# A hybrid decoder step on one core: the triangular inverse of the gated-delta mixing loop grown in place, and its TensorE work reordered

## The chip, the cores and the metric

The kernel runs on one core of one Trainium2 chip. The metric is the device time of one execution in microseconds (us), lower is better. All data is float32.

## What is computed

One layer for 1024 prompt tokens and 8 sampled tokens: RMSNorm, one input projection, two groups of mixing heads (sliding-window attention with 8 query and 2 key heads; a gated DeltaNet with 8 heads of width 64), output projection and residual, a mixture of experts, a gated embedding, a last norm. The change is in the prompt's mixing, and there in the DeltaNet, per head and per chunk of 64 tokens:

```
gam   = cumsum(g)
decay = exp(where(causal, gam_i - gam_j, -inf))
A     = where(strict, (k*beta) k^T * decay, 0)
sol   = triangular_solve(I + A, [v*beta, k*beta*exp(gam)])       # u, w
v_new = u - w S
o     = (q*exp(gam)) S + where(causal, q k^T * decay, 0) v_new
S     = S*exp(gam_last) + (k*exp(gam_last - gam))^T v_new
```

## The kernel before

The program has stages, each a block of five engine programs that meet at semaphores: projection and convolution (to about 360 us), mixing (365 to 899), routing and experts (to 1357), the last stage. The mixing stage works on tiles of 128 prompt tokens. A tile holds two chunks of 64 tokens, one in the lower and one in the upper 64 partitions (`HB`), and all 8 heads stand side by side (slots of 64 columns). The first tile is written out ahead of the loop (`first=True`; it also carries the output projection of the 8 sampled tokens), the other seven are one loop body, `Fori(1, NT)`, on every engine.

The body is skewed. Attention scores, decay sums, Gram matrices and the inverse are those of tile t; the end of the DeltaNet of tile t-1 (`solve_first`, `carry`, `solve_second`, `outputs`, `increments`, `turn_out`) and the output projection of tile t-1 (`project`, 8 parts k, each 128 rows of the weight for two times 512 columns) stand between them. A hand-written order on TensorE (from L1430) is what places the work; the other engines' orders are written to match. Semaphores count once per tile or per level, and eight PSUM banks are shared by hand.

In each tile, of what the change touches:
- TensorE computes the running sums of g into banks 4 to 6 (L1443 to L1445). VectorE subtracts them (L1178, `E_`), GpSimd adds a mask of -1e30 (L1038), ScalarE takes the exponential (L1306).
- q and k are turned to token rows (L1451), squared on ScalarE (L1299), summed and completed on VectorE (L1183 to L1186); GpSimd raises 16 columns to -0.5 (L1027, `rms_pow("qk")`).
- VectorE forms `gU = E_ * bet` (L1198), and `ATd`, the two 64x64 diagonal blocks of the transposed A (L1203), `ATo`, the off-diagonal block (L1206).
- The inverse: with `MT` the transposed inverse of the block diagonal of I + A and `T_` its transpose, a level l doubles the block size. `Lo` is ATd under the level's mask, made on GpSimd (L1050; level 0 on VectorE, L1205). A level is X = Lo' T (TensorE, L1495), X to SBUF (ScalarE, L1322), P = M' X (L1502) and PT = X' M (L1510), then T and MT of the next level by subtraction (VectorE, L1162, two halves of four heads each for T and for MT, into the other of two buffers). LV = 5 levels, so 28 products over four heads, each eight 64x64 multiplications (`quarters`, L1427). T of level 0 is MT turned by TensorE against the identity (L1485) and copied by ScalarE (L1318).
- In between: the query-key products QK (L1469, bank 0), v turned to rows (L1475, bank 7), the output of tile t-1 turned (L1395, `turn_out`, waits for `og` of VectorE, L1119), the state products (L1516, after level 2), the rows of the residual turned for the router (L1407, after level 4), then the softmax shares turned (L1526), the router's logits (L1414) and the attention values (L1537).
- SyncE's queue loads the next tile's queries and keys after the second scores, x after `h` (the residual sum, L1125), the convolved rows after the state products, the attention values after `av_ps`, the gate rows after `gz`.

Every float32 multiplication appears in the trace as two records, a turn on TensorE (`transpose`) as one. `settle` only increments a semaphore of its own.

## Time and profile before

| | us |
|---|---|
| median of 3 runs | 1496.92 (1495.38 to 1507.93) |
| the profiled execution | 1497.95 |
| its span, first to last instruction | 1496.1 |
| TensorE busy | 1319.2 |
| VectorE busy | 621.4 |
| ScalarE busy | 377.0 |
| GpSimd busy | 257.0 |

The engines are PE (TensorE multiplications), PEld (its weight loads), DVE (VectorE), ACT (ScalarE), POOL (GpSimd) and SP (SyncE, which starts transfers). Busy shares of the whole span mix stages; what concerns this change is between 365 and 899 us. A duration of PE is modelled to the end of its pipeline, so neighbouring records overlap: what a block of records takes is the distance from its start to the start of the next. PEclk is the granted TensorE clock, 1.00 being 2.4 GHz and 0.50 being 1.2 GHz.

### The profile page before, as it was taken

What the parts mean: (1) busy time and instruction counts of PE and PEld (TensorE: products, weight loads), DVE (VectorE), ACT (ScalarE), POOL (GpSimd) and SP (SyncE); (2) the same over time, 40 slices, a digit from 0 to 9 for tenths busy, and PEclk for the clock granted to TensorE, in tenths of its full rate; (3) what the DMA queues carried; (4) which work ended last, traced back from release to release, by engine and by line L of the source; (5) the groups of instructions that cost most, each with busy time, mean ns of one, the idle gap of its engine ahead of it and who ended that gap; (6) DMA issues with size and microseconds to landing.
All of it is one profiled execution on the core that took longest, in us unless ns stands there. A gap on an engine that the chain in (4) does not pass through costs nothing. (4 is left out here: it accounts for less than half of the span.)

```text
span 1496.1 us, 24403 instructions
## 1 busy us (share of the span) xinstructions
PE 1319.2 (88%) x9660; PEld 920.9 (62%) x9660; DVE 621.4 (42%) x1050; ACT 377.0 (25%) x743; POOL 257.0 (17%) x299
## 2 busy tenths in 40 slices
PE   6999999954889898898988966899999999993987
PEld 4669999933567586685765834344544454442876
DVE  2324454047654655646656317021121111116464
ACT  2322232120424233243332311211111111113332
POOL 0000000021321232213322100112222222200110
PEclk9999999965989999999999977899999999996999
DMA  6211323066102112011120108669999999955451
GB/s 199 85 50 59 110 84 113 17 152 191 39 25 69 38 49 84 25 67 49 49 74 11 42 32 310 255 227 338 342 351 339 345 358 352 323 223 211 141 172 44
DMA packets 151338, 226.12 MB, mean 151 GB/s; under 512 B 12651, under 2 KB 123835, under 8 KB 146670
## 3 DMA queue, kind: packets, MB, share of 16 engines
q1 hardware_dynamic: 130606, 171.27, 34.2%
q10 hardware_dynamic: 11184, 28.48, 5.4%
q0 software_dynamic: 9504, 25.77, 4.4%
q8 instruction: 30, 0.49, 0.1%
q14 instruction: 14, 0.11, 0.0%
HBM read 183.37 MB, written 46.76 MB: 154 GB/s over the span
## 5 line engine op out<-in xcount | busy, mean ns | idle before, releaser
L1661 PE MATMUL psum<-experts 128*128 128x512 f32 x528 | 235.2, 599 | 2.6 <-DVE experts L1683 2.6
L627 PE MATMUL psum<-split_parts 128*128 128x344 f32 x1224 | 194.1, 321 | 0.0
L627 PEld LDWEIGHTS psum<-split_parts 128*128 128x128 f32 x1224 | 193.9, 188 | 0.1
L1661 PEld LDWEIGHTS psum<-experts 128*128 128x128 f32 x528 | 101.2, 192 | 130.5 <-issue 127.2
L1427 PE MATMUL psum<-decode_and_mix 64*64 64x64 f32 x3584 | 121.2, 221 | 10.1 <-ACT decode_and_mix L1322 5.4
L1698 DVE COPY experts<-psum 128x256 f32<-128x256 f32 x33 | 14.0, 425 | 275.0 <-PE psum L1668 275.0
L1401 PE MATMUL psum<-decode_and_mix 128*128 128x512 f32 x256 | 127.3, 655 | 0.7 <-ACT decode_and_mix L1283 0.7
L1427 PEld LDWEIGHTS psum<-decode_and_mix 64*64 64x64 f32 x3584 | 113.7, 136 | 16.8 <-issue 14.5
L1677 PE MATMUL psum<-experts 128*128 128x512 f32 x264 | 119.3, 594 | 1.5 <-ACTq L1714 1.0
L2264 PE MATMUL psum<-last_parts 128*128 128x512 f32 x432 | 101.1, 394 | 0.0
L1401 PEld LDWEIGHTS psum<-decode_and_mix 128*128 128x128 f32 x256 | 53.6, 216 | 63.6 <-issue 62.0
L2264 PEld LDWEIGHTS psum<-last_parts 128*128 128x128 f32 x432 | 81.3, 190 | 16.6
L1162 DVE TENSOR_TENSOR decode_and_mix<-decode_and_mix,psum 128x256 f32<-128x256 f32 x144 | 60.6, 421 | 56.4 <-PE psum L1427 51.1
L1645 POOL DMA_INDIRECT ye_d<-experts x33 | 33.3, 1008 | 271.8 <-ACT experts L1712 268.0
L1677 PEld LDWEIGHTS psum<-experts 128*128 128x128 f32 x264 | 47.6, 190 | 49.3 <-issue 47.3
L1027 POOL TENSOR_TENSOR decode_and_mix<-decode_and_mix,lasting 128x16 f32<-128x16 f32 (+3 forms) x25 | 41.4, 1657 | 188.6 <-DVE decode_and_mix L1129 149.1
L1712 ACT ACTIVATE experts<-psum 128x1024 f32<-128x1024 f32 x33 | 33.8, 1024 | 138.9 <-PE psum L1677 138.9
L1050 POOL TENSOR_TENSOR decode_and_mix<-decode_and_mix,lasting 128x512 f32<-128x512 f32 x40 | 56.4, 1417 | 44.9 <-PE psum L1427 23.2
L587 PE MATMUL psum<-project 128*128 128x512 f32 x144 | 64.0, 597 | 0.0
L1705 ACT ACTIVATE experts<-psum 128x256 f32<-128x256 f32 x33 | 12.7, 385 | 200.7 <-PE psum L1661 200.7
L1683 DVE TENSOR_TENSOR experts<-psum,lasting 128x1024 f32<-128x1024 f32 x33 | 40.4, 1224 | 52.7 <-PE psum L1653 52.7
L422 DVE SCALAR_TENSOR_TENSOR project<-project 128x1056 f32<-128x1056 f32 x36 | 47.5, 1319 | 4.7 <-DVE project L418 1.5
(371 smaller groups left out, 1715.7 us busy)
## 6 DMA issues: line engine op xcount, KB each, us to landing
experts<-in_w_gate SPq DMA_DIRECT2D x33, 1024.0 KB, 5.8
experts<-in_w_up SPq DMA_DIRECT2D x33, 1024.0 KB, 10.6
experts<-in_w_down SPq DMA_DIRECT2D x33, 1024.0 KB, 12.3
project<-in_w_in SPq DMA_DIRECT2D x18, 512.0 KB, 5.0
last<-ye_d SPq DMA_DIRECT2D x16, 512.0 KB, 6.9
conv_out_d<-project ACTq DMA_DIRECT2D x12, 512.0 KB, 3.1
decode_and_mix<-conv_out_d SPq DMA_DIRECT2D x8, 768.0 KB, 4.8
until_mixed<-in_x_prompt SPq DMA_DIRECT2D x8, 512.0 KB
```

The lines of the kernel that those rows point to most:

```text
L422: nc.vector.scalar_tensor_tensor(yc[:, u, 0:NV], xp[:, u, j:j + NV], cwT[:, ft, j:j + 1], yc[:, u, 0:NV], ALU.mult, ALU.add).then_inc(S(f" ...
L587: mm = nc.tensor.matmul(bank(5 + 2 * u), xT[:, u, k, :], wtok[:, k, 144:], start=(k == 0), stop=(k == KD - 1))
L627: mm = nc.tensor.matmul(thirds(u)[:, b], w[:, u, k, :], x[:, k, b * TB:(b + 1) * TB], start=(i == 0 and k == 0), stop=(i == 2 and k == KD ...
L1027: g.tensor_tensor(out, in_, half[0:out.shape[0]].to_broadcast([out.shape[0], n]), ALU.pow).then_inc(S("r_" + name), 1)
L1050: g.tensor_tensor(Lo[l % 2], ATd, bm(cst[:, C_LV + l * P:C_LV + l * P + HD], NH), ALU.mult).then_inc(S("Lo"), 1)
L1162: V.tensor_tensor(bufs[l % 2][:, hs], bufs[(l - 1) % 2][:, hs], four(src + g), ALU.subtract).then_inc(S(f"{n}{g}"), 1)
L1401: mm = T.matmul(bank(2 + n)[0:R], src[:, k, :], wout[:, k, n * 512:(n + 1) * 512], start=(k == 0), stop=(k == KD - 1))
L1427: mm = T.matmul(bank(out + g)[HB[b], (s % 4) * HD:(s % 4 + 1) * HD], left[HB[b], s, :], right[HB[b], s, :], start=True, stop=True)
L1661: mm = nc.tensor.matmul(bank(2 + s.v), xgT[s.v][:, k, :], wgu[s.u][:, k, :], start=(k == 0), stop=(k == KD - 1))
L1677: mm = nc.tensor.matmul(bank(6 + n), hT[s.v][:, k, :], wd[s.u][:, k, n * 512:(n + 1) * 512], start=(k == 0), stop=(k == KE - 1))
L1683: nc.vector.tensor_tensor(xgT[s.v], flat(0, 2).rearrange("p (k c) -> p k c", c=P), bc(g_ffn, P), ALU.mult).then_inc(S("xgT" + s.h), 1)
L2264: mm = nc.tensor.matmul(bank(4 + 2 * (t % 2) + m), x[t % 2][:, k, :], w[:, k, cols], start=(i == 0 and k == 0), stop=(i == 2 and k == KD - 1))
```

## The change

The inverse keeps one buffer each for MT and T_. Per level, the product X uses the whole (negated) ATd, there is no P product, and a masked copy (`copy_predicated`) writes the level's entries of PT into MT; T_ is MT with each 32x32 block turned by VectorE. Level 0 is copied straight from ATd into a unit matrix that GpSimd writes. `beta` is applied to ATd with its sign (`betn`), not to E_. The decay difference is eight `tensor_scalar` per head with a minimum of 0 in the place of the mask, and GpSimd multiplies with a 0/1 mask into `Em`, for QK alone. The q and k norms are computed apart. v is turned early and copied by ScalarE to `vraw`. On TensorE the projection is cut into two, two, two and two parts; QK, `turn_out` and the state products stand between the levels; the last turns of the tile are now those of the shares, then the values of half 0, `turn_rows`, the values of half 1 and `route`. ScalarE's end of the tile is the copy of the turned shares 0, `store_rows`, shares 1, `turned_rows`, the values. VectorE's products with the state products (`tmpk`, `tmp`) stand before `fill(t, 4)`, `r_` and the decay of `Sst` behind `residual`.

```diff
-        kqS_ps = flat(2, 2).rearrange("p (a n f e) -> p a n f e", a=2, n=2, f=4)
+        kqS_ps = flat(4, 2).rearrange("p (a n f e) -> p a n f e", a=2, n=2, f=4)
...
                 def tile(t, first=False):
-                    g.wait_ge(S("v_D"), t + 1)
-                    g.tensor_tensor(E_, E_, bm(cst[:, C_NEG:C_NEG + P], NH), ALU.add).then_inc(S("D"), 1)
-                    rms_pow("qk", r16, m16, 16, t)
                     if not first:
                         gate(t - 1)
+                        g.wait_ge(S("v1_ps"), t)
+                    settle(g)
+                    g.tensor_copy(MT, bm(cst[:, C_EYE:C_EYE + HD], NH)).then_inc(S("eye"), 1)
+                    rms_pow("k", r16[:, NH:], m16[:, NH:], NH, t)
+                    if not first:
                         rms_pow("o", r8, m8, NH, t - 1)
-                    for l in range(1, LV + 1):
...
-                        g.tensor_tensor(Lo[l % 2], ATd, bm(cst[:, C_LV + l * P:C_LV + l * P + HD], NH), ALU.mult).then_inc(S("Lo"), 1)
...
+                    rms_pow("q", r16[:, 0:NH], m16[:, 0:NH], NH, t)
+                    g.wait_ge(S("E"), t + 1)
+                    g.tensor_tensor(Em, E_, bm(cst[:, C_U:C_U + P], NH), ALU.mult).then_inc(S("Em"), 1)
+                    R = DEC if first else P
+                    rms_pow("x", rsx[0:R], msx[0:R], 1, t)
 
                 def next_sums(t, n):
-                    g.wait_ge(S("ATo"), t + 1)
+                    g.wait_ge(S("gam_ps"), t + 1)
                     sums(n)
...
-                def subtract(t, l, name, bufs, count, src, n):
+                def fill(t, l):
+
                     for g in range(2):
                         hs = slice(4 * g, 4 * g + 4)
-                        v.wait_ge(S(f"{name}{g}_ps"), count)
-                        V.tensor_tensor(bufs[l % 2][:, hs], bufs[(l - 1) % 2][:, hs], four(src + g), ALU.subtract).then_inc(S(f"{n}{g}"), 1)
+                        if l == 0:
+                            v.wait_ge(S("ATn"), t + 1)
+                            v.wait_ge(S("eye"), t + 1)
+                        else:
+                            v.wait_ge(S(f"PT{g}_ps"), LV * t + l)
+                        settle(v)
+                        mask = cst[:, C_LV + l * P:C_LV + l * P + HD].bitcast(I32)
+                        V.copy_predicated(MT[:, hs], bm(mask, 4), ATd[:, hs] if l == 0 else four(6 + g)).then_inc(S(f"MT{g}"), 1)
+                        if l < LV:
+                            v.wait_ge(S(f"MT{g}"), (LV + 1) * t + l + 1)
+                            V.transpose(T_[:, hs].rearrange("p h d -> p (h d)"), MT[:, hs].rearrange("p h d -> p (h d)")).then_inc(S(f"T{g}"), 1)
...
+                    largest(t, 0)
...
-                    V.tensor_tensor(E_, gB, bc(gam8, P), ALU.subtract).then_inc(S("v_D"), 1)
                     V.tensor_tensor(kdec, gB[:, :, P - 1], gam8, ALU.subtract).then_inc(S("kd_in"), 1)
+                    for h in range(NH):
+                        ins = V.tensor_scalar(E_[:, h], gB[:, h], gam8[:, h:h + 1], 0.0, ALU.subtract, ALU.min)
+                    ins.then_inc(S("D"), 1)
                     if not first:
                         outputs(t - 1)
...
                     if not first:
                         state(t - 1)
                         gated(t - 1)
-                    largest(t, 0)
-                    v.wait_ge(S("r_qk"), t + 1)
+                    v.wait_ge(S("r_k"), t + 1)
...
+                    V.scalar_tensor_tensor(betn, rk2, -1.0, gb[:, t, 0:NH], ALU.mult, ALU.mult).then_inc(S("v_betn"), 1)
                     V.tensor_tensor(bet, rk2, gb[:, t, 0:NH], ALU.mult).then_inc(S("v_bet"), 1)
-                    V.tensor_tensor(gU, E_, bc(bet, P), ALU.mult).then_inc(S("Eb"), 1)
...
-                        V.tensor_tensor(ATd[HB[b]], G[HB[b], :, HB[b]], gU[HB[b], :, HB[b]], ALU.mult).then_inc(S("ATd"), 1)
+                        V.tensor_tensor(ATd[HB[b]], G[HB[b], :, HB[b]], E_[HB[b], :, HB[b]], ALU.mult).then_inc(S("ATd"), 1)
...
+                    V.tensor_tensor(ATd, ATd, bc(betn, HD), ALU.mult).then_inc(S("ATn"), 1)
...
+                    fill(t, 0)
                     if not first:
                         gated_out(t - 1)
+                    largest(t, 1)
+                    fill(t, 1)
+                    v.wait_ge(S("QK_ps"), t + 1)
+                    v.wait_ge(S("Em"), t + 1)
+                    V.tensor_tensor(QK, flat(4, 2).rearrange("p (h i) -> p h i", i=P), Em, ALU.mult).then_inc(S("QK"), 1)
+                    fill(t, 2)
+                    v.wait_ge(S("vraw"), t + 1)
+                    v.wait_ge(S("v_kab"), t + 1)
+                    V.tensor_tensor(vtok, vraw, bc(kab, HD), ALU.mult).then_inc(S("vtok"), 1)
+                    denominators(t, 0)
+                    fill(t, 3)
+                    denominators(t, 1)
...
+                    fill(t, 4)
                     residual(t, R)
...
+                    fill(t, 5)
+                    mean_rows(t, R)
                     logits(t, R, dst)
...
                     A.activation(sq, flat(0, 2), ACT.Square).then_inc(S("sq"), 1)
-                    act.wait_ge(S("kd_in"), t + 1)
+                    act.wait_ge(S("tokv_ps"), t + 1)
+                    A.activation(vraw, heads(bank(2)), ACT.Copy).then_inc(S("vraw"), 1)
+                    act.wait_ge(S("D"), t + 1)
...
                     exponentials(t, 0)
...
                             A.activation(Xs[:, 4 * g:4 * g + 4], four(g), ACT.Copy).then_inc(S(f"X{g}"), 1)
                         if l == 1:
-                            norm_rows(t, R, rows)
+                            exponentials(t, 1)
                         if l == 2:
+                            if not first:
+                                mix_rows(t - 1)
+                        if l == 3:
                             shares(t, 0)
-                        if l == 3:
-                            store_rows(t, R, rows)
                         if l == 4:
                             shares(t, 1)
-                    turned_rows(t, R)
+                        if l == 5:
+                            norm_rows(t, R, rows)
...
+                def level(t, l):
+                    for g in range(2):
+                        pe.wait_ge(S(f"T{g}"), LV * t + l)
+                        quarters(g, 0, ATd, T_).then_inc(S(f"X{g}_ps"), 1)
+                    for g in range(2):
+                        pe.wait_ge(S(f"X{g}"), LV * t + l)
+                        quarters(g, 6, Xs, MT).then_inc(S(f"PT{g}_ps"), 1)
...
+                    mm.then_inc(S("tokv_ps"), 1)
                     if not first:
                         outputs(t - 1)
-                    pe.wait_ge(S("kd_in"), t + 1)
+                    pe.wait_ge(L("wout"), 16)
+                    pe.wait_ge(S("vraw"), t + 1)
+                    project(R, src, 0, 2)
+                    pe.wait_ge(S("D"), t + 1)
...
                         increments(t - 1)
-                    project(R, src, 0, 4)
+                    project(R, src, 2, 4)
...
+                    if not first:
+                        pe.wait_ge(S("S"), t + 1)
+
+                    level(t, 1)
...
                     mm.then_inc(S("QK_ps"), 1)
+                    level(t, 2)
+                    pe.wait_ge(S("QK"), t + 1)
                     if not first:
                         turn_out(t - 1)
+                    level(t, 3)
...
+                    mm.then_inc(S("kS_ps"), 1)
+                    project(R, src, 4, 6)
+                    level(t, 4)
+                    project(R, src, 6, 8).then_inc(S("proj_ps"), 1)
+                    level(t, 5)
...
+                        if g == 0:
+                            pe.wait_ge(S("h"), t + 1)
+                            turn_rows(t, R)
                     mm.then_inc(S("av_ps"), 1)
+                    route(t, R)
```

## Rows read from the trace of the kernel before

**Rows 1.** The page's first part: busy us and share of each engine

```profile
PE 1319.2 (88%) x9660; PEld 920.9 (62%) x9660; DVE 621.4 (42%) x1050; ACT 377.0 (25%) x743; POOL 257.0 (17%) x299
```

**Rows 2.** Timeline of TensorE, first iteration, last one's start: start, us, engine, line, records

```profile
421.10 1.14 PE L1362 MATMUL psum<-decode_and_mix 64*64 64x64 f32 x16
...
428.54 1.04 PE L1451 MATMUL psum<-lasting,decode_and_mix 128*128 128x128 f32 x8
429.41 1.90 PE L1383 MATMUL psum<-decode_and_mix 128*128 128x64 f32 x16
...
432.94 7.13 PE L1401 MATMUL psum<-decode_and_mix 128*128 128x512 f32 x16
...
446.19 1.12 PE L1395 MATMUL psum<-lasting,decode_and_mix 128*128 128x128 f32 x4 [5.02 <-DVE decode_and_mix L1119]
...
448.91 8.56 PE L1401 MATMUL psum<-decode_and_mix 128*128 128x512 f32 x16
457.39 1.15 PE L1485 MATMUL psum<-lasting,decode_and_mix 64*64 64x64 f32 x32
458.61 4.31 PE L1427 MATMUL psum<-decode_and_mix 64*64 64x64 f32 x128
...
465.12 2.00 PE L1516 MATMUL psum<-decode_and_mix 64*128 64x64 f32 x32
...
477.20 1.97 PE L1526 MATMUL psum<-lasting,decode_and_mix 128*128 128x128 f32 x16
...
482.70 0.50 PE L1362 MATMUL psum<-decode_and_mix 64*64 64x64 f32 x5
...
851.40 1.14 PE L1362 MATMUL psum<-decode_and_mix 64*64 64x64 f32 x16
```

**Rows 3.** Window of the second iteration: us, busy PE, PEld, DVE, ACT, POOL, PEclk

```profile
482.70:543.90 61.20, 54.60 (x766) 41.59 (x766) 36.01 (x71) 21.86 (x54) 17.52 (x11) 0.94 0.16 54
```

**Rows 4.** Windows around falls of the clock, same columns

```profile
406.00:410.00 4.00, 1.86 (x57) 1.63 (x54) 1.73 (x4) 2.35 (x6) 1.02 (x1) 1.00 0.26 72
410.00:412.00 2.00, 2.00 (x47) 1.93 (x42) 1.27 (x3) 0.00 (x0) 0.00 (x0) 0.75 0.03 8
441.20:446.20 5.00, 0.01 (x1) 0.01 (x1) 4.84 (x7) 0.00 (x0) 2.97 (x2) 0.89 0.13 44
446.20:453.00 6.80, 6.11 (x14) 3.33 (x15) 3.35 (x6) 2.13 (x8) 0.00 (x0) 0.58 0.00 0
853.00:855.00 2.00, 1.11 (x16) 1.00 (x16) 0.70 (x2) 0.00 (x0) 0.00 (x0) 0.94 0.00 0
```

**Rows 5.** Groups of instructions, 430 to 850 us: busy us, mean ns of one, idle before

```profile
L1162 DVE TENSOR_TENSOR decode_and_mix<-decode_and_mix,psum 128x256 f32<-128x256 f32 x126 | 53.1, 421 | 46.4 <-PE psum L1427 41.7
...
L1288 ACT ACTIVATE decode_and_mix<-decode_and_mix 128x256 f32<-128x256 f32 x56 | 27.8, 497 | 46.2 <-DVE decode_and_mix L1150 46.2
L1322 ACT ACTIVATE decode_and_mix<-psum 128x256 f32<-128x256 f32 x70 | 26.9, 384 | 57.6 <-PE psum L1427 54.4
```

**Rows 6.** Timelines of VectorE and GpSimd, first loop iteration

```profile
428.94 1.22 DVE L1178 TENSOR_TENSOR decode_and_mix<-psum,decode_and_mix 128x1024 f32<-128x1024 f32 x1
...
434.34 0.69 DVE L1105 TENSOR_REDUCE decode_and_mix<-decode_and_mix 128x8 f32<-128x512 f32 x1 [0.58 <-ACT decode_and_mix L1262]
...
436.59 1.11 DVE L1147 TENSOR_TENSOR decode_and_mix<-decode_and_mix,lasting 128x4 f32<-128x4 f32 x1
...
439.65 1.41 DVE L1203 TENSOR_TENSOR decode_and_mix<-psum,decode_and_mix 64x512 f32<-64x512 f32 x2
...
443.63 1.78 DVE L1116 TENSOR_TENSOR decode_and_mix<-decode_and_mix 128x512 f32<-128x512 f32 x1
...
436.41 1.27 POOL L1034 TENSOR_TENSOR decode_and_mix<-decode_and_mix,lasting 128x512 f32<-128x512 f32 x1
```

**Rows 7.** Groups of GpSimd in the loop: busy us, mean ns

```profile
L1038 POOL TENSOR_TENSOR decode_and_mix<-decode_and_mix,lasting 128x1024 f32<-128x1024 f32 x7 | 16.5, 2357 | 144.1 <-DVE decode_and_mix L1178 144.1
L1027 POOL TENSOR_TENSOR decode_and_mix<-decode_and_mix,lasting 128x8 f32<-128x8 f32 x7 | 11.5, 1645 | 0.0
```

More of the change, by code:

```diff
@@ L951, in program @@
         QK = mem.take(NH, P)
-        Lo = [mem.take(NH, HD) for _ in range(2)]
-        Xs = mem.take(NH, HD)
-        T_ = [mem.take(NH, HD) for _ in range(2)]
-        MT = [mem.take(NH, HD) for _ in range(2)]
+        Em = mem.take(NH, P)
+        Xs, T_, MT = (mem.take(NH, HD) for _ in range(3))
         sq = mem.take(2 * NH * HD)
@@ L961, in program @@
         ss16, m16, r16 = mem.take(16), mem.take(16), mem.take(16)
-        ss8, m8, r8, egam, kdec, eglS, gam8, rqp, rq2, bet, rk2, kab = (mem.take(NH) for _ in range(12))
+        ss8, m8, r8, egam, kdec, eglS, gam8, rqp, rq2, bet, betn, rk2, kab = (mem.take(NH) for _ in range(13))
         mx, mm_, nm_, es_, den, rcp = ([mem.take(GQA) for _ in range(2)] for _ in range(6))
@@ L1312, in tile @@
                     exponentials(t, 0)
-                    if not first:
-                        mix_rows(t - 1)
-                    exponentials(t, 1)
-                    for g in range(2):
-                        act.wait_ge(S(f"T0{g}_ps"), t + 1)
-                        A.activation(T_[0][:, 4 * g:4 * g + 4], four(g), ACT.Copy).then_inc(S(f"T0{g}"), 1)
                     for l in range(1, LV + 1):
@@ L1470, in tile @@
                     mm.then_inc(S("QK_ps"), 1)
+                    level(t, 2)
+                    pe.wait_ge(S("QK"), t + 1)
                     if not first:
                         turn_out(t - 1)
+                    level(t, 3)
+                    if not first:
                         pe.wait_ge(S("mixB"), t)
-                    for f in range(4):
-                        mm = T.transpose(slots(heads(bank(7)))[:, :, f, :], yst[:, 8 + f, :], ident)
-                    mm.then_inc(S("tokv_ps"), 1)
@@ new lines, in tile @@
+                    pe.wait_ge(S("S"), t + 1)
+                    for n in range(2):
+                        for h in range(NH):
+                            mm = T.matmul(kqS_ps[:, h % 2, n, h // 2, :], yst[half_of(h), 4 - 4 * n + h // 2, :], Sst[half_of(h), h // 2, :], start=True, stop=True)
+                    mm.then_inc(S("kS_ps"), 1)
[3 more added lines that the diff above has]
+                    level(t, 5)
@@ L1522, in tile @@
                     for g in range(2):
                         pe.wait_ge(S(f"pn{g}"), t + 1)
+                        if g == 1:
+                            for i in range(2):
+                                pe.wait_ge(S(f"MT{i}"), (LV + 1) * t + LV + 1)
                         for i in range(GQA):
                             for b in range(2):
[L1526 removed]
+                                mm = T.transpose(flat(6 * g, 2)[:, (2 * i + b) * P:(2 * i + b + 1) * P], sA[g][:, i, b * P:(b + 1) * P], ident)
```

147 lines of the change are left out of this document (41 added, 106 removed).

## Prediction

> **What bounds the kernel now.** I read the page's busy shares first: TensorE is busy 88% of the span, VectorE 42% [rows 1]. Then the mixing loop alone. One iteration is one 128-token tile; TensorE starts it with the first half of the triangular solve at 421.10, the next at 482.70, the last at 851.40 [rows 2], so (851.40 - 482.70) / 6 = 61.45 us each. In an iteration TensorE is busy 54.6 us, VectorE 36.0, ScalarE 21.9, GpSimd 17.5 [rows 3]. The timeline of TensorE [rows 2] shows three things:
> - a dense stretch of small multiplications (the levels, 458.61 to 477.20),
> - one hole of 5.02 us before L1395, which waits for VectorE's `og`, and 0.7 us behind it,
> - what follows the hole runs slowly: the second half of the projection takes 8.56 us where the same 16 records of the first half take 7.13, and four turns take 1.12 where eight took 0.87 (428.54 to 429.41).
> The windows say why: the granted clock is 0.89 in the hole and 0.58 on the 6.8 us behind it [rows 4]. Its levels are 1.00 and 0.50, 2.4 and 1.2 GHz: 0.89 over 5.0 us is 1.1 us at the lower one before 446.2, 0.58 over 6.8 is 5.8 after, so it lasts from 445.1 to 452.0. It costs 8.56 - 7.13 = 1.4, and about 0.5 on each of the two groups of four turns: 2.5 us or so. So TensorE bounds the iteration: 61.45 = 52.7 of work at full clock + 2.5 clock + 5.7 hole and wait + 0.5 small gaps.
>
> **The change part by part.** Times from here count from the start of `solve_first`.
>
> (1) *Removed on TensorE.* The P products (2 groups in 4 levels = 8 groups of 8 multiplications) and the first turn of MT (16 multiplications, L1485). 128 records (8 groups of 16) of L1427 take 462.92 - 458.61 = 4.31, so a group is 0.54 and the P products 4.3; the turn, from 457.39 to 458.5, is 1.1 [rows 2]. Work becomes 52.7 - 5.4 = 47.3.
>
> (2) *The 5 us hole.* `turn_out` now stands behind level 2, long after `og`. The hole, the 0.7 behind it and the 2.5 of clock go: 8.2. If nothing replaced them an iteration would take 61.45 - 5.4 - 8.2 = 47.9. The rest is what is late next.
>
> (3) *New VectorE instructions.* No row shows a masked copy or a 32x32 turn. Each works on 128x256. The nearest row is the 128x256 `tensor_tensor` from PSUM that they replace: 0.42 [rows 5]. The bounds are nothing below and a 128x1024 operation above (1.22, L1178) [rows 6]. I take 0.42. A fill of one level is copy, turn, copy, turn: 4 x 0.44 = 1.8 with the 0.03 from one end to the next dependent start. Eight 128x128 `tensor_scalar` from PSUM replace L1178's 1.22 plus GpSimd's mask (2.36 [rows 7]): by the slope between 256 and 1024 elements (0.80 / 768 = 1.04 ns each) one is 0.28, pitch 0.21 as neighbours overlap by 0.07; 1.7 in all, bounds nothing and 0.42 each, so up to 3.4. It stands beside the projection and costs nothing up to there. Whole load of VectorE: minus 18 subtractions, Lo0, gU, two first MT, D (about 12.5), plus 12 copies, 10 turns, ATn, D (about 12.7): still 36, no bound by its sum.
> The Trainium skill (VectorE: DVE Perf Modes, "The three transpose paths") gives 311 ns for VectorE's turn of 128x128 in bf16. No run here shows it; by the slope above 256 elements would take 0.44, which leaves the sum alone if fp32 runs at that rate, and the page has no fp32 price.
>
> (4) *Until level 1.* The five blocks solve, scores, carry, scores, solve and the decay sums end at 428.54 - 421.10 = 7.4, eight turns at 8.3 [rows 2]; the four turns of v, now here, at 8.75. `outputs`, G and `increments` take 3.5 together (429.41 to 432.94): 1.8, 1.1, 0.6. So `outputs` ends at 10.6; projection 0-1 (half of the 7.1 for four k) 14.1; G 15.2; `increments` 15.8; projection 2-3 19.4. Its waits are met: ScalarE has copied v by about 10 and VectorE D by 11.1. TensorE then needs T of level 0. VectorE: state(t-1) waits for the increments until 15.95 (they now stand behind two k of the projection), then state 0.42, gated 1.0 (a 0.69 reduction as L1105, two small ones), the small products 0.5, two halves of ATd 1.4 (L1203), ATn 0.7 and ATo 0.6 [rows 5, 6]: fill 0 begins at 20.45, T of heads 0-3 is there at 21.35. The new unit copy (1.27 as L1034) waits in GpSimd's queue for the second solve (5.5); behind it stand only pows, the first wanted at 12.8, so it is free. New hole: 1.97.
>
> (5) *GpSimd against fill 0.* GpSimd's order is pow k, pow o (from 17.4), pow q, then Em, a 128x1024 product of 2.36. At 1.65 per pow of 8 columns Em starts at 20.65; its 2.36 is L1038's [rows 7]. Rows show such instructions excluding each other: the 128x4 L1147 takes 1.11 and ends at 437.70, as GpSimd's `gz` (L1034) does at 437.68; L1116 takes 1.78 where its size takes 0.69 (L1105) [rows 6]. Both have two SBUF inputs. The pows I take as free of it. Fill 0's copies read ATd and the mask, both in SBUF. The first copy runs before Em; the second waits for Em's end at 23.2, and T of heads 4-7 is there at 24.15, not 22.2. TensorE does one group at 21.35 and waits from 21.9 to 24.15: 2.25. Bounds: 0 to 2.4.
> The Trainium skill (GPSIMD Engine Reference, "Specifications") says that VectorE instructions with two SBUF inputs contend with GpSimd; L1147's 1.11 agrees. It would not hold later fills, whose data lie in PSUM, which leaves the sum as it is.
>
> (6) *Levels.* At full clock level 1 ends at 25.8, QK 26.9. VectorE does gated_out to 25.6, largest(1) (1.6) to 27.2, then fill 1: T at 28.1 and 28.95. TensorE idles 1.2 + 0.3; ScalarE does four exponentials of half 1 (4 x 0.50 and 0.19, less overlap: 2.15) from 27.25 to 29.4 and only then level 2's copy of X (0.38) [rows 5]: 0.35 more. Level 2 ends at 30.95, turn_out 31.4, level 3 (0.25 gap) 33.85. Now the fillers cover: state products 2.0 (L1516), projection 4-5 3.55 beside fill 3; level 4, projection 6-7 beside fill 4, end 45.15. Level 5 begins there.
>
> (7) *Tail.* Level 5 2.16, shares, routing and values as now 5.5 (477.20 to 482.70), row turns 1.1 (eight, as L1451) [rows 2]: 8.8, with 0.7 of waits, since residual, squares, pow, scale and turn of the rows now follow each other behind the last projection. 45.15 + 9.45 = 54.6. SP's conv load waits, in its queue, for `h` behind it: issued at 46.4, needed 15.6 later, so free; the query load is behind `gz`, done early.
>
> (8) *Clock.* From 19.4 to 24.15 TensorE works 0.54 of 4.75. In the first tile it was busy 1.86 of the 4 us to 410, and the clock fell in the next 2 (0.75) though it was busy again [rows 4]. So I expect the lower level from about 23, until a dense stretch lifts it: behind the hole it took 3 us of unbroken work, from 448.91 to 452. TensorE is unbroken from 24.15, so about 29.5. Levels 1 and QK double to end at 29.5, but VectorE and ScalarE held level 2 until nearly then: it ends at 31.7 where it ended at 30.95. Cost 0.8. Iteration: 55.4.
>
> **The sum.** 61.45 - 55.4 = 6.05, seven times 42. The first tile has no og hole and no gated_out; the P products and the turn go (5.4), its low clock (about 2.5) too, against 1.7 before level 1 and 1 to 2 in the levels: 4. The tail behind the loop keeps its order. 1497.95 (the profiled execution, span 1496.1) - 46 = 1452; the median of the runs shown is 1496.92, 1 below, the same for this purpose. Forecast 1452.
>
> **Rivals.**
> - *Clock and port do no harm.* For it: the loop's old levels keep it. Against: [rows 4, 6]. Without (8) 54.6, total 1446; without (5) too, 52.4, total 1428. Chance 0.15.
> - *The fills are dearer, 0.69 each.* Fills 0 to 2 stand on the path with two, four and four operations, the last with about one: 11 x 0.27 = 3.0 an iteration, 8 times, 24: 1476. Chance 0.14.
> - *The clock stays low through levels 2 and 3.* TensorE must then do QK, level 2, turn and level 3 at half speed: level 3 ends at 39.15 instead of 34.65, state products 2 late: 4.5 more, 36 in all: 1488. For it: behind the loop `solve_first`, `carry` and `solve_second` stand with gaps of 0.9 between them, and the clock falls there too (853 to 855: busy 1.11 of 2, clock 0.94) [rows 4]. Against: from 24.15 TensorE is almost unbroken. Chance 0.13.
> - *Slower: VectorE becomes the bound of the levels.* If copy and turn both take the 1.22 of a 128x1024 operation (a quarter of the rate), 11 x 0.80 = 8.8, and fill 4 (4.9) outlasts its 3.55 of projection: 10.3 an iteration against a gain of 6.05; eight times, 1452 + 82 = 1534. It turns to a loss where 8 x 11 x the excess is the 46 us gained: from 0.42 + 0.52 = 0.94 each. For it: no row for either. Against: the row of that size stands at 0.42 with the same kinds of operands [rows 5]. Chance 0.11.
> - *The change is made but another wait (a buffer, SP's queue) holds each tile for 5 us.* 1492. Nothing in the rows names one: 0.02.
> The forecast itself (1444 to 1466) has 0.45.
>
> **How the numbers follow.** A run of this kernel can tell about 1% (15 us) from no change. Faster than 1482: forecast, first and second rival and a bit of the third, 0.77. Within 1%: most of the third and the fifth, 0.13. Slower by over 1%: 0.10. The range 1428 to 1488 takes in the first three rivals and leaves out the slower one and the edges.
>
> **What would show it.** Right: L1427 at 2560 records, not 3584; iteration 55 to 56; no wait for `og` before the turns; an idle of 2 us before level 1 of each tile and about as long inside it; the first two masked copies of a tile unequal, the second some 2 us long beside Em; clock low for 5 to 7 us around level 1. Wrong: masked copies or turns above 0.6, low clock beyond level 2, or TensorE waiting in levels 4 and 5.

## The result and the profile after

The changed kernel's median is 1458.24 us, the kernel before 1500.4 on the same chip (four executions each). The ratio is 0.969, 95% interval 0.961 to 0.976. One of the four took 7197 us; it is left out of the ratio, for which a fifth of 1449.70 stands in, and the median of these four is 1450.4. Seven more executions on another chip gave 1457.78 (1449.20 to 1461.55) against 1504.68, ratio 0.970 (0.967 to 0.974). The forecast was 1452.

The page of the changed kernel, profiled execution of 1465.40 us, busy line and the groups of the new operations:

```profile
span 1463.6 us, 21846 instructions
PE 1291.1 (88%) x8380; PEld 890.4 (61%) x8380; DVE 616.3 (42%) x1130; ACT 375.8 (26%) x735; POOL 209.9 (14%) x275
...
L1431 PE MATMUL psum<-decode_and_mix 64*64 64x64 f32 x2560 | 103.7, 234 | 36.8 <-DVE decode_and_mix L1166 29.3
...
L1163 DVE COPY_PREDICATED decode_and_mix<-lasting,psum 128x256 f32<-128x256 int32 x80 | 33.4, 428 | 49.6 <-PE psum L1431 49.6
```

TensorE's busy share is the same 88% (1291.1 of 1463.6) as in [rows 1]: work and span both fell, by 28.1 and 32.5 us. The level multiplications have 2560 records: 20 products over four heads in a tile where there were 28, 16 records each, 8 tiles. Of the 36.8 us of idle time ahead of them 29.3 end with VectorE's turn (L1166): that is the new limit. The group of that turn in the loop (430 to 820 us):

```profile
L1166 DVE STREAM_TRANSPOSE decode_and_mix<-decode_and_mix 128x256 f32<-128x256 f32 x70 | 31.2, 446 | 2.4
```

Stages of the profiled executions, from the starts of TensorE's blocks (us; "again" is the changed kernel's second profiled execution, on another chip):

| stage | before | after | again |
|---|---|---|---|
| up to mixing | 365.8 | 366.8 | 367.2 |
| first tile | 55.3 | 55.0 | 48.4 |
| the seven loop iterations | 430.3 | 401.2 | 391.8 |
| block behind the loop, to the end of mixing | 48.4 | 48.3 | 48.2 |
| routing, experts | 456.9 | 452.0 | 451.6 |
| last stage | 139.4 | 140.3 | 140.2 |
| span | 1496.1 | 1463.6 | 1447.4 |

The 851.40 of [rows 2] is the start of the block behind the loop, not of a last iteration, so that 430.3 are seven iterations. They were 61.45 each before (the first 61.60). After: 59.10, 62.16, 55.67, 56.39, 55.68, 56.56, 55.68. Again: 56.30, 55.66, 56.56, 55.68, 55.68, 56.26, 55.68. The same program has iterations of several kinds. The shortest, 55.68, is called undisturbed here; in it the granted clock is low for 3.4 us. In those of 56.3 to 56.6 it is low for 6.8 us at the same place (621.40 to 628.20 in the fourth). The two longest, 59.10 and 62.16, are taken up below.

TensorE in the third iteration (start, us, engine, line, records, idle before and its releaser), to be laid beside [rows 2]:

```profile
543.09 1.14 PE L1367 MATMUL psum<-decode_and_mix 64*64 64x64 f32 x16
...
558.86 3.70 PE L1405 MATMUL psum<-decode_and_mix 128*128 128x512 f32 x8
564.67 0.68 PE L1431 MATMUL psum<-decode_and_mix 64*64 64x64 f32 x16 [2.11 <-DVE decode_and_mix L1166]
567.16 2.83 PE L1431 MATMUL psum<-decode_and_mix 64*64 64x64 f32 x48 [1.81 <-DVE decode_and_mix L1166]
569.91 1.26 PE L1493 MATMUL psum<-decode_and_mix 64*128 64x128 f32 x16
571.16 2.74 PE L1431 MATMUL psum<-decode_and_mix 64*64 64x64 f32 x64
573.83 0.66 PE L1399 MATMUL psum<-lasting,decode_and_mix 128*128 128x128 f32 x4
574.62 2.74 PE L1431 MATMUL psum<-decode_and_mix 64*64 64x64 f32 x64
...
588.81 2.40 PE L1431 MATMUL psum<-decode_and_mix 64*64 64x64 f32 x64
...
598.76 0.44 PE L1367 MATMUL psum<-decode_and_mix 64*64 64x64 f32 x4
```

The wait of 5.02 for `og` of [rows 2] is gone: the turns of L1399 now have none. Two holes have come, 2.11 before level 1 and 1.81 inside it. VectorE and GpSimd in the same stretch show why:

```profile
559.05 0.42 DVE L1089 TENSOR_TENSOR decode_and_mix<-decode_and_mix,psum 128x256 f32<-128x256 f32 x1 [2.57 <-PE psum L1393]
...
563.62 0.43 DVE L1163 COPY_PREDICATED decode_and_mix<-lasting,decode_and_mix 128x256 f32<-128x256 int32 x1
564.08 0.45 DVE L1166 STREAM_TRANSPOSE decode_and_mix<-decode_and_mix 128x256 f32<-128x256 f32 x1
564.45 2.09 DVE L1163 COPY_PREDICATED decode_and_mix<-lasting,decode_and_mix 128x256 f32<-128x256 int32 x1
566.57 0.45 DVE L1166 STREAM_TRANSPOSE decode_and_mix<-decode_and_mix 128x256 f32<-128x256 f32 x1
```

```profile
563.75 2.49 POOL L1045 TENSOR_TENSOR decode_and_mix<-decode_and_mix,lasting 128x1024 f32<-128x1024 f32 x1
```

VectorE idles 2.57 until the increments (L1393) are there. Its first masked copy takes 0.43; the second starts while GpSimd's product `Em` (L1045) runs, until 566.24, and ends at 566.54, 0.3 behind it. TensorE's second group of level 1 can only start after the turn that follows.

### The profile page after: what moved, and what is told of

Read it like the earlier page. It is cut to its first block and busy times, and to the rows that moved or that the text cites. A ratio compares the mean times of both kernels' runs of the same rounds, so it can differ in the third digit from the quotient of the medians.

```text
span 1463.6 us, 21846 instructions
## 1 busy us (share of the span) xinstructions
PE 1291.1 (88%) x8380; PEld 890.4 (61%) x8380; DVE 616.3 (42%) x1130; ACT 375.8 (26%) x735; POOL 209.9 (14%) x275
## 5 line engine op out<-in xcount | busy, mean ns | idle before, releaser
L1658 PE MATMUL psum<-experts 128*128 128x512 f32 x528 | 232.2, 592 | 2.6 <-DVE experts L1680 2.6
L1658 PEld LDWEIGHTS psum<-experts 128*128 128x128 f32 x528 | 100.2, 190 | 128.3 <-issue 125.3
L1431 PE MATMUL psum<-decode_and_mix 64*64 64x64 f32 x2560 | 103.7, 234 | 36.8 <-DVE decode_and_mix L1166 29.3
L1431 PEld LDWEIGHTS psum<-decode_and_mix 64*64 64x64 f32 x2560 | 92.7, 146 | 64.1 <-issue 62.9
L1405 PE MATMUL psum<-decode_and_mix 128*128 128x512 f32 x256 | 121.1, 618 | 0.7 <-ACT decode_and_mix L1288 0.7
L1025 POOL TENSOR_TENSOR decode_and_mix<-decode_and_mix,lasting 128x8 f32<-128x8 f32 (+2 forms) x33 | 44.1, 1344 | 334.3 <-DVE decode_and_mix L1123 231.1
L1405 PEld LDWEIGHTS psum<-decode_and_mix 128*128 128x128 f32 x256 | 47.7, 196 | 51.6 <-issue 49.1
L1674 PEld LDWEIGHTS psum<-experts 128*128 128x128 f32 x264 | 47.6, 190 | 49.2 <-issue 47.3
L1322 ACT ACTIVATE decode_and_mix<-psum 128x256 f32<-128x256 f32 x80 | 30.6, 383 | 138.1 <-PE psum L1431 136.0
L1163 DVE COPY_PREDICATED decode_and_mix<-lasting,psum 128x256 f32<-128x256 int32 x80 | 33.4, 428 | 49.6 <-PE psum L1431 49.6
```

Of the source, the lines that this page charges most:

```text
L1025: g.tensor_tensor(out, in_, half[0:out.shape[0]].to_broadcast([out.shape[0], n]), ALU.pow).then_inc(S("r_" + name), 1)
L1163: V.copy_predicated(MT[:, hs], bm(mask, 4), ATd[:, hs] if l == 0 else four(6 + g)).then_inc(S(f"MT{g}"), 1)
L1405: mm = T.matmul(bank(2 + n)[0:R], src[:, k, :], wout[:, k, n * 512:(n + 1) * 512], start=(k == 0), stop=(k == KD - 1))
L1431: mm = T.matmul(bank(out + g)[HB[b], (s % 4) * HD:(s % 4 + 1) * HD], left[HB[b], s, :], right[HB[b], s, :], start=True, stop=True)
L1658: mm = nc.tensor.matmul(bank(2 + s.v), xgT[s.v][:, k, :], wgu[s.u][:, k, :], start=(k == 0), stop=(k == KD - 1))
L1674: mm = nc.tensor.matmul(bank(6 + n), hT[s.v][:, k, :], wd[s.u][:, k, n * 512:(n + 1) * 512], start=(k == 0), stop=(k == KE - 1))
```

## Experiments

Each is an edit of the changed kernel; the code shown is cut to what matters. There are twelve runs on three chips, each beside the kernel before. "Steady" is the length of the undisturbed loop iteration in the trace.

### Em earlier on GpSimd

```diff
 rms_pow("k", ...)
+g.wait_ge(S("E"), t + 1)
+g.tensor_tensor(Em, E_, ...).then_inc(S("Em"), 1)
 if not first:
     rms_pow("o", r8, m8, NH, t - 1)
 rms_pow("q", ...)
-g.wait_ge(S("E"), t + 1)
-g.tensor_tensor(Em, E_, ...).then_inc(S("Em"), 1)
```

> Only GpSimd's order changes: Em is made before the pows of the outputs and of q, while VectorE waits for the state increments. Theory of the shared access: the second masked copy of level 0, 2.09 us in the changed kernel, falls to 0.43, T of heads 4-7 comes 1.7 us sooner, each iteration gets 1.7 to 2.4 us shorter (55.7 to about 53.6), 8 tiles: about 16 us below the changed kernel's 1450, so 1434. Rival: a masked copy with both data and mask in SBUF is simply slow, or the turn in front of it holds it up: it stays near 2 us and nothing is gained, 1450. The hole of 2.1 us before level 1 stays in both.

Steady 54.00, 1.68 less. Em now runs while VectorE waits for the increments, and both masked copies of fill 0 are short (the second was 2.09):

```profile
605.61 0.43 DVE L1163 COPY_PREDICATED decode_and_mix<-lasting,decode_and_mix 128x256 f32<-128x256 int32 x1
...
606.44 0.40 DVE L1163 COPY_PREDICATED decode_and_mix<-lasting,decode_and_mix 128x256 f32<-128x256 int32 x1
```

So the second hole is Em's doing; the first, ahead of level 1, is still 2.11. The kernel's median is 1457.13 and the ratio 0.972 (0.967 to 0.978), no better than the changed kernel's: its four executions lie in two pairs, 1447 to 1449 and 1466 to 1468. The end of this part comes back to that.

### Increments earlier on TensorE

```diff
     outputs(t - 1)
+    pe.wait_ge(S("v_gC"), t + 1)
+    increments(t - 1)
 ...
 project(R, src, 0, 2)
 ...
-if not first:
-    increments(t - 1)
 project(R, src, 2, 4)
```

> Only TensorE's order changes: the state increments stand right behind the outputs, in front of projection parts 0 and 1. Theory: VectorE no longer waits 2.6 us for them, ATd and fill 0 come 2.5 us sooner, so the hole of 2.1 us before level 1 goes and level 1 begins behind the projection; Em now collides with fill 0 as before, so the first heads' T may still be late. Iteration 55.7 to about 53.2, total about 1430. Rival: the chain to level 1 is set by the pow of k or by D, and not by the increments: hole stays, 1450.

Steady 53.78, where 53.2 was expected; median 1444.15, ratio 0.959 (0.955 to 0.963). Fill 0 starts earlier and its first copy now meets Em. The hole inside level 1 is gone, and the one ahead of it is still 1.76, of Em's making now (VectorE, then TensorE):

```profile
604.30 1.87 DVE L1163 COPY_PREDICATED decode_and_mix<-lasting,decode_and_mix 128x256 f32<-128x256 int32 x1
...
606.57 0.40 DVE L1163 COPY_PREDICATED decode_and_mix<-lasting,decode_and_mix 128x256 f32<-128x256 int32 x1
```

```profile
606.79 2.73 PE L1431 MATMUL psum<-decode_and_mix 64*64 64x64 f32 x64 [1.76 <-DVE decode_and_mix L1166]
```

### Both

The two edits above together.

> Both moves. Theory: no wait of TensorE before level 1 or inside it, the granted clock stays at 1.00 through the levels, level 2 ends about 4.2 us sooner (what holds it next is VectorE's maximum and ScalarE's exponentials of the second heads), iteration 55.7 to about 51.4, total about 1450 - 34 = 1416. Rival, the work behind level 2 has slack of its own and gives only half: 1433.

A miss: steady 53.48, only 0.30 below the increments alone; median 1447.62, ratio 0.963 (0.961 to 0.966). The two engines met elsewhere. VectorE, then GpSimd:

```profile
550.50 2.32 DVE L1102 TENSOR_TENSOR decode_and_mix<-decode_and_mix 128x8 f32<-128x8 f32 x1
```

```profile
550.43 2.36 POOL L1042 TENSOR_TENSOR decode_and_mix<-decode_and_mix,lasting 128x1024 f32<-128x1024 f32 x1
```

A product of 128x8, 0.17 at 560.10 in the changed kernel, takes 2.32, and everything up to fill 0 stands behind it; the hole ahead of level 1 is 1.45. Em is a block of 2.4 us that has to lie where VectorE issues nothing that excludes it.

### Em late, increments early

```diff
 g.wait_ge(S("E"), t + 1)
+g.wait_ge(S("nm1"), t + 1)
 g.tensor_tensor(Em, E_, ...).then_inc(S("Em"), 1)
```

and the increments as in the second experiment. `nm1` is VectorE's second maximum, behind fill 0.

> Both GpSimd and TensorE changed: the increments behind the outputs, ahead of the projection, and GpSimd's 128x1024 product waits until VectorE has taken the maxima of the second half, so that it runs beside none of VectorE's instructions with two SBUF inputs of fill 0. Theory (the port that GpSimd and VectorE share is what is left of the hole in front of and inside level 1: 2.32 us on the 128x8 product of the run with both): both holes go, the steady iteration is 51.0 to 52.0 us and the kernel 1425 to 1432. Rival (GpSimd's product meets other VectorE instructions later, or the exponentials wait): 53 to 54 us, 1440 to 1450, no better than the increments alone.

Steady 52.65, above the 51.0 to 52.0 expected but the shortest of all. The median is 1442.11, ratio 0.958 (0.954 to 0.962), where 1425 to 1432 was expected and the rival had 1440 to 1450; the changed kernel on the same chip has 1457.78. VectorE, then GpSimd, then TensorE:

```profile
596.31 0.43 DVE L1164 COPY_PREDICATED decode_and_mix<-lasting,decode_and_mix 128x256 f32<-128x256 int32 x1
...
601.11 0.45 DVE L1164 COPY_PREDICATED decode_and_mix<-lasting,psum 128x256 f32<-128x256 int32 x1
...
601.96 0.41 DVE L1164 COPY_PREDICATED decode_and_mix<-lasting,psum 128x256 f32<-128x256 int32 x1
...
603.73 1.22 DVE L1223 TENSOR_TENSOR decode_and_mix<-psum,decode_and_mix 128x1024 f32<-128x1024 f32 x1 [0.88 <-POOL decode_and_mix L1046]
```

```profile
601.27 2.35 POOL L1046 TENSOR_TENSOR decode_and_mix<-decode_and_mix,lasting 128x1024 f32<-128x1024 f32 x1 [5.81 <-DVE decode_and_mix L1145]
```

```profile
597.37 2.73 PE L1432 MATMUL psum<-decode_and_mix 64*64 64x64 f32 x64 [0.31 <-DVE decode_and_mix L1167]
600.03 1.16 PE L1494 MATMUL psum<-decode_and_mix 64*128 64x128 f32 x16
602.18 2.74 PE L1432 MATMUL psum<-decode_and_mix 64*64 64x64 f32 x64 [0.99 <-DVE decode_and_mix L1167]
```

The hole before level 1 is 0.31. Fill 1's second copy, whose data lie in PSUM, takes 0.41 with Em running all the while; the first, 0.45, began 0.16 before Em. What is left is 0.99 before level 2, where VectorE comes late from its maxima. This kernel and that of the second experiment were then run again, on one chip:

> The kernel of e2_increments_early again, beside that of e7_em_late on one chip. Expected: steady iteration 53.8, about 0.960 of the kernel before.

> The kernel of e7_em_late again, beside e11. Theory (its undisturbed iteration is 1.1 us shorter, seven times): 8 us below e11, about 0.955 of the kernel before. Rival (the stretches of lower clock that come at some iteration boundaries with TensorE fully busy, 5 to 6 us each, decide): the two differ by less than 0.3%.

Increments alone: 1443.12, ratio 0.962 (0.957 to 0.967). With Em late: 1437.71, ratio 0.956 (0.951 to 0.960), 5.4 us below where the steady iterations (53.78 and 52.64) promise 8. The intervals overlap. So that Em late is better than the increments alone is shown by the iterations, not by the medians. Both beat the changed kernel's 0.970 (0.967 to 0.974), and with Em late clearly so.

### The P products put back

```diff
+if l < LV:
+    for g in range(2):
+        pe.wait_ge(S(f"X{g}"), LV * t + l)
+        quarters(g, 6, MT, Xs)
 for g in range(2):
     pe.wait_ge(S(f"X{g}"), LV * t + l)
     quarters(g, 6, Xs, MT).then_inc(S(f"PT{g}_ps"), 1)
```

> The changed kernel with the removed P products put back as work alone (their result is overwritten by PT), 8 groups of 0.54 us a tile, in levels 1 to 4 between X and PT. Theory: the levels are one chain, X to SBUF to PT to the masked copy to T, so all of it is added although TensorE has waits in these levels: 3.8 to 4.3 us a tile, 8 tiles, total 1480 to 1485. Rival: the waits of TensorE in levels 1 to 3 take up the work, and the busier TensorE keeps its clock: at most 2 us a tile, 1466 or less.

Median 1488.70, ratio 0.990 (0.986 to 0.994), above the 1480 to 1485 expected. Iterations alternate between 59.28 and 60.14, as the clock is low for 3.4 or 6.8 us in them; against 55.68 and 56.4 of the changed kernel that is 3.6 to 3.75, where 0.94 of products came back in each of four levels (3.34 - 2.40, 3.8 in all): nearly all of it is on the path. TensorE, level 4, whose group has 96 records where it had 64 in 2.40:

```profile
650.51 3.34 PE L1431 MATMUL psum<-decode_and_mix 64*64 64x64 f32 x96
```

### The spreading undone

```diff
-level(t, 1)
 ... QK ...
+if not first:
+    turn_out(t - 1)
+    pe.wait_ge(S("mixB"), t)
+project(R, src, 4, 8).then_inc(S("proj_ps"), 1)
+level(t, 1)
 level(t, 2)
 pe.wait_ge(S("QK"), t + 1)
-if not first:
-    turn_out(t - 1)
-level(t, 3)
-if not first:
-    pe.wait_ge(S("mixB"), t)
 ... state products ...
-project(R, src, 4, 6)
+level(t, 3)
 level(t, 4)
-project(R, src, 6, 8).then_inc(S("proj_ps"), 1)
 level(t, 5)
```

ScalarE copies the turned output ahead of the levels (`mix_rows`), and the turns go to bank 7 in place of 4. VectorE's order stays that of the changed kernel.

> The spreading undone and the rest of the change kept: the turn of the outputs, projection 4 to 7 and the wait for them stand ahead of level 1, and the state products behind level 2, so levels 3, 4 and 5 follow each other with nothing between them. Theory (the fills of 1.8 us that start levels 3 to 5 are covered only by what is put between the levels): about 1.3 to 1.5 us are uncovered in front of each of levels 3, 4 and 5, some 4 us, while the projection now covers the 2.1 us in front of level 1; with the wait for og behind the values that comes back in part (the turn is ahead of level 1, where og is long awaited) an iteration takes 58 to 61 us and the kernel 1475 to 1500. Rival (TensorE's sum of work sets the end and the order is of no matter): 55 to 56.5 us an iteration, 1455 to 1462.

Median 1503.53, ratio 0.999 (0.996 to 1.002): just above the 1475 to 1500 expected, and no gain at all is left. The steady iteration is 61.2 to 61.45 (two others of the profiled execution, 65.2 and 67.6, hold more low clock). TensorE:

```profile
698.75 0.91 PE L1398 MATMUL psum<-lasting,decode_and_mix 128*128 128x128 f32 x4 [3.57 <-DVE decode_and_mix L1113]
700.34 9.84 PE L1404 MATMUL psum<-decode_and_mix 128*128 128x512 f32 x16 [0.69 <-ACT decode_and_mix L1288]
...
713.27 2.73 PE L1430 MATMUL psum<-decode_and_mix 64*64 64x64 f32 x64 [0.76 <-DVE decode_and_mix L1166]
...
721.03 2.73 PE L1430 MATMUL psum<-decode_and_mix 64*64 64x64 f32 x64 [0.76 <-DVE decode_and_mix L1166]
724.21 2.74 PE L1430 MATMUL psum<-decode_and_mix 64*64 64x64 f32 x64 [0.45 <-DVE decode_and_mix L1166]
```

A hole like the old one is back: 3.57 for the gated outputs, 0.69, and half a projection in 9.84 where 7.13 is usual [rows 2]. It is not wholly the old one, for VectorE now makes `og` behind fill 0, whose second copy still takes 2.09 beside Em. Between bare levels the fills show only 0.45 to 0.76 each, 2.0 in all, not the 1.3 to 1.5 expected three times. What I had wrong there is where the loss would sit. The turns of the output begin 25.5 into the iteration (25.1 before), so what was removed could only shorten what follows. There the rows show, against the kernel before, 2.0 of waits for the fills, 2.2 of levels that take 2.40 to 2.74 in place of the 2.16 reckoned, 1.4 of slower projection and about 1.0 more in the tail. So the removed products and the removed hole are not two gains to be added at will: shorter levels on TensorE's old placement give nothing.

### Every masked copy twice

```diff
+V.copy_predicated(MT[:, hs], ...).then_inc(S(f"cc{g}"), 1)
+v.wait_ge(S(f"cc{g}"), (LV + 1) * t + l + 1)
+settle(v)
 V.copy_predicated(MT[:, hs], ...).then_inc(S(f"MT{g}"), 1)
```

> Every masked copy is made twice, with a wait of its own between, so each of the 12 of a tile costs 0.45 to 0.5 us more. Theory (the copies of fills 0, 1 and 2 stand on the path of the end, those of fills 3, 4 and the last behind 3.6 us of projection and behind the tail): 0.5 to 1.0 in fill 0 (the second copy waits for GpSimd anyway), 1.0 and 1.0 in fills 1 and 2, so 2.5 to 3.0 in an iteration: 58.2 to 58.7, and 1478 to 1482 for the kernel. Rival 1 (VectorE is nearly the bound in all the levels): 4 to 5 more in an iteration, 1490 or above. Rival 2 (other waits end later than the copies): up to 1 more, 1466 or below.

The four executions took 1484.74, 1508.64, 1529.52 and 1484.77 us; the trace is of the first. Steady is 59.84, 4.16 more than 55.68, which is above the 2.5 to 3.0 expected. By its trace a doubled copy costs 0.55 to 0.59. Counted from the iteration's start, the end of level 3 moved from 34.3 to 37.7, and no more was lost up to level 5 (45.7 to 49.2); 0.7 came at the end:

```profile
652.24 1.07 PE L1522 MATMUL psum<-lasting,decode_and_mix 128*128 128x128 f32 x8 [1.02 <-DVE decode_and_mix L1166]
```

So fills 0 to 2 are on the path (3.46) and fills 3 and 4 are covered by the projection, as forecast. Fill 5 is on it too, which I had at nothing: the turn of the second half of the shares waits for MT.

### Holes filled with work

```diff
 for g in range(2):
+    if l == 1:
+        for _ in range((5, 5)[g]):
+            T.matmul(bank(g), ones, wout[:, 0, 0:512], start=True, stop=True)
     pe.wait_ge(S(f"T{g}"), LV * t + l)
     quarters(g, 0, ATd, T_).then_inc(S(f"X{g}_ps"), 1)
```

> TensorE gets ten more multiplications of 128x512 in each tile, whose results nobody reads: five ahead of each of the two X groups of level 1, in the two holes there, about 1.1 us in each of the holes of 2.1 and 1.8 us. Theory (the two holes lower the granted clock behind them, and that costs 0.5 to 0.8 us in an iteration): the clock is 1.00 around level 1, an iteration is 0.3 to 0.8 us shorter (54.9 to 55.4) and the kernel 2 to 6 us faster. Rival 1 (the lower clock there is hidden behind VectorE and ScalarE): same time, at a clock of 1.00. Rival 2 (the hole is no longer there to be filled, or the clock falls all the same): the added work costs up to 1 to 2 us an iteration, 1465 to 1475.

> As e6_filled, with two added multiplications of 128x512 ahead of each X group of level 1 in place of five: each took 0.90 us there, not the 0.22 that was reckoned, so that ten of them overran the holes of 2.1 and 1.8 us. Two take 1.8 and should just fill one hole. Theory (the lower clock behind the holes costs an iteration 0.5 to 1.3 us): granted clock 1.00 around level 1, steady iteration 54.4 to 55.3. Rival (the lower clock is hidden): 55.6 to 56.0 at a clock of 1.00. The kernel's time can't tell them apart well (4 to 10 us), the steady iterations of the trace can.

The first was mis-sized by me: a float32 multiplication of this size takes 0.9 (five in 4.46), so the holes were overrun; steady 59.05, 1482.18 and ratio 0.987 (0.983 to 0.992). With two in each hole (median 1455.20, ratio 0.968, 0.962 to 0.973) the granted clock is 1.00 in the first six iterations, and the window of a steady iteration is this (us, busy PE, PEld, DVE, ACT, POOL, PEclk):

```profile
529.90:585.60 55.70, 52.98 (x616) 37.36 (x615) 35.39 (x81) 21.68 (x53) 11.61 (x8) 1.00 0.19 59
```

Steady 55.68, exactly that of the changed kernel, where the window of the third iteration has 0.97 and the stretch behind the holes 0.50:

```profile
543.09:598.76 55.67, 50.48 (x607) 37.07 (x607) 35.37 (x81) 21.69 (x53) 11.61 (x8) 0.97 0.19 59
...
568.00:570.00 2.00, 2.00 (x40) 1.88 (x36) 1.93 (x5) 0.38 (x1) 0.00 (x0) 0.50 0.00 0
```

The rival holds: in iterations like the third, the lower clock costs nothing. Those where it is low for 6.8 us, as the fourth, are 0.6 to 0.9 longer. What TensorE gains in level 1 it waits for in front of level 2: 0.94 for VectorE's turn, where the changed kernel has none. Added work of 3.9 us on TensorE (1.88 and 1.98 in its timeline) was free as well.

### The changed kernel again

No edit.

> The changed kernel itself, once more beside the kernel before and beside the three that follow, for their comparison on one chip. Theory: about 0.97 of the kernel before; iterations 3 to 7 at 55.7 to 56.5 us, iteration 2 about 62 (a stop of TensorE for 1.7 us with nothing to wait for late in iteration 1, and the lower clock for some 17 us behind it). Rival: that stop was an accident of the one profiled execution; then iteration 2 takes about 57 here.

The rival held. There was no stop of 1.70 and no iteration of 62. This explains most of the difference between forecast and profile. The first profiled execution shows two stops of TensorE with nothing to wait for, and the lower clock behind each:

```profile
396.31 1.55 PE L1431 MATMUL psum<-decode_and_mix 64*64 64x64 f32 x24 [2.03 <-issue]
397.79 3.68 PE L1505 MATMUL psum<-decode_and_mix 64*128 64x64 f32 x32
...
478.43 2.57 PE L1418 MATMUL psum<-decode_and_mix 128*128 128x36 f32 x12 [1.70 <-issue]
```

```profile
478.00:494.00 16.00, 15.57 (x82) 11.94 (x82) 7.27 (x13) 0.00 (x0) 0.61 (x1) 0.50 0.19 62
```

L1505 takes 3.68 for what takes 2.00 at full clock, and TensorE is busy for 15.57 of the window of 16 us (same columns as above) at 0.50. The second execution has neither stop, and its first tile is 6.7 us shorter, its first two iterations 2.8 and 6.5. The kernel before had such stops too, both in the first tile of its profiled execution:

```profile
397.92 2.64 PE L1427 MATMUL psum<-decode_and_mix 64*64 64x64 f32 x72 [1.54 <-issue]
...
409.52 1.61 PE L1427 MATMUL psum<-decode_and_mix 64*64 64x64 f32 x48 [2.04 <-issue]
```

Such stretches of low clock also come without a stop. The kernel with filled holes, windows ahead of and in its long sixth iteration:

```profile
700.00:714.00 14.00, 13.40 (x153) 10.21 (x152) 4.48 (x11) 7.32 (x12) 3.66 (x3) 1.00 0.58 177
714.00:728.00 14.00, 14.00 (x75) 9.90 (x74) 8.51 (x19) 0.00 (x0) 0.61 (x1) 0.53 0.17 57
```

TensorE was busy 13.40 of 14 us, and fell to the lower level all the same. A stretch of nearly 14 us has one price: 65.43 - 59.05 = 6.4 here, 62.05 - 55.68 = 6.4 with the holes filled less, 60.16 - 53.78 = 6.4 with the increments early, 59.00 - 52.65 = 6.4 with Em late. Others differ: one of 10 us cost 4.7 (57.34 - 52.64, Em late), and the iterations right behind a stop, with 14 to 17 us of low clock, were 5.4 to 7.3 longer. The kernel before had one among its experts (10 us from 956 at 0.56). Laid beside the trace of the changed kernel from the start of the stage, it has lost 4.84 us by the 25th record of the experts' product L1661 (L1658 after), at 977, and 0.13 more up to the end: this is the 4.9 that its routing and experts stage is longer, though nothing in it changed. With none, one or two such stretches in an execution, two kernels whose steady iterations promise 12 and 13 us (Em early, increments early) came out 1 and 14 below the changed kernel. What sets them off was not found.

## Why the prediction was right, and where it was off

Forecast 1452, range 1428 to 1488; measured 1458.24 and 1457.78. Against the second execution, which has no iteration above 56.6, the sum was 1496.1 - 46 = 1450.1 of span, and 1447.4 was measured. Part of this nearness is luck: of the 48.7 gained there, 45.4 are the loop and the first tile, which the sum is about, and 5.3 came from routing and experts, where nothing changed.

- *(1) Removed work.* Confirmed: 2560 records, and putting the products back costs 3.6 to 3.75 us an iteration against the 4.3 reckoned: two groups more in a level take 0.94, 0.47 each, not 0.54. That the turn of MT (1.1) was worth its time was not tested apart.
- *(2) The hole of 5 us with its clock.* Confirmed: gone after the change, and one of 3.57 + 0.69 + 2.7 of slow projection = 7.0, against 8.2, is there when the spreading is undone, in part of another making.
- *(3) Prices.* Masked copy 0.428 and turn 0.446 against 0.42 each. The rival with 0.69 and the slower rival (a loss from 0.94 each) fall by these two rows. So does the rival with a low clock through levels 2 and 3, by the clock at 1.00 again from 570.2 in the third iteration and from 628.2 in the fourth. The eight small decay operations took 2.15, not 1.7, and are covered.
- *(4) The hole before level 1.* 2.11 against 1.97, of the cause named (VectorE idles 2.57 for the increments). Moving the increments alone leaves 1.76, because Em then falls on the first copy; with Em moved behind fill 0 as well, 0.31 is left.
- *(5) GpSimd against fill 0.* 1.81 against 2.25, with the second copy at 2.09 beside Em; moving Em takes it away. That later fills would be free of it is shown by the copy beside Em (0.41).
- *(6), (7) Levels and tail.* At full clock a level takes 2.40, not 2.16, some 0.24 more in each. Level 5 began at 45.7 against 45.15. Of the 1.5 of waits expected in front of level 2, 0.94 is there with the holes filled; otherwise the slow level 1 takes it up. The tail was 9.95 against 9.45, level 5 itself (2.40 for 2.16) being half of that excess.
- *(8) The clock.* Low for 3.4 us in the third iteration, 6.8 in the fourth, against 6.5 expected. The 29.5 at which it was to end did not follow from what stood there: 3 us of unbroken work from 24.15 is 27.2, and it ended at 27.1 in the third iteration, 29.4 in the fourth. Its cost in the sum, 0.8, was wrong for the steady iteration: 0 with the clock held at 1.00. I had seen that VectorE and ScalarE hold level 2 and still charged the rest. For the iterations with the longer stretch it was about right: the fourth is 0.7 longer (56.39), the sixth 0.9.
- *Iteration:* 55.68 against 55.4, so 5.8 saved against 6.05.

The terms that were mis-sized are the loop's 42, which was 29.1 in the first execution and 38.5 in the second, and the first tile's 4, which was 0.2 and 6.9. In the first execution both lost what the stops and the stretches of low clock took: 6.7 in the tile, and about 9.3 in the first two iterations. The 6.9 of the second holds something that the sum left out: the two stops of 3.6 in the first tile of the kernel before, of which 0.7 is there in the second execution. The stage of the experts gave 4.9 back, since the profile of before had such a stretch there. The sum was made against one profiled execution as if each stage's time were fixed; each may hold a stretch of 5 to 7 us that nothing in the order explains.

## What to carry to other kernels

When removed work and reordered work go together, ask which of the two exposes the next wait: here the removal was worth 3.6 us an iteration with the new order on TensorE and nothing with TensorE's placement put back near the old one. A GpSimd product on large SBUF tiles is a block in time for VectorE: place it beside VectorE's idle time or instructions that it was seen to leave alone (the copies on PSUM data, the turns), and look again after every other move, since the neighbour changes. And compare lengths of undisturbed loop iterations before medians: they tell 0.3 us of 55 apart where the medians of whole executions do not tell 5 of 1450.

## What was not expected of the hardware

- VectorE's turn of 32x32 blocks on 128x256 float32 takes 0.446 and a copy under an integer mask 0.428, both about as much as an ordinary 128x256 operation [rows 5].
- GpSimd's 128x1024 product held up a 128x8 operation for the whole of its length (2.32 for 0.17), but neither a copy whose data lay in PSUM (0.41) nor the turn between the copies (0.45). Its powers of 128x8 (1.6 each) held up nothing seen here: VectorE's product of 128x512 from SBUF (L1213) took its 0.69 beside one of them. The Trainium skill (GPSIMD Engine Reference, "Specifications") says that VectorE instructions with two SBUF inputs contend with GpSimd; the copy from SBUF under a mask in SBUF agrees (2.09), the powers do not show it.
- GpSimd's broadcast copy of 128x512 takes 0.61, half of its 1.27 for a product of that size [rows 6].
- The granted clock fell to 0.50 for some 13 us although TensorE had been busy 13.4 of the 14 us before, at a cost of 6.4 us, in some executions of a program and not in others. The forecast had low clock only behind idle time.
- TensorE stops of 1.4 to 2.0 us with nothing to wait for, in the first tile or at the end of the first iteration, which one execution of the program has and another has not.
